# Experts in another order of work: two small mixture-of-experts layers of one transformer kernel, ordered by a table

## What is computed

```
def _hierarchical_moe(h, w_group, w_expert, w_gate, w_up, w_down):
    group = jnp.argmax(group_prob, axis=-1)                  # one of 4 groups
    top_p, top_local = lax.top_k(softmax(exp_logits), TOP_K)  # 2 of its 8 experts
    ...
    def expert_block(args):
        xb, e = args
        return (jax.nn.silu(xb @ w_gate[e]) * (xb @ w_up[e])) @ w_down[e]
    ...                                # rows of one expert at a time, then
    contrib = y[dest] * w_sorted[:, None]      # weighted sum of a token's two rows
```

## Time and profile before

| | |
|---|---|
| median of three runs | 3255.23 us |
| profiled execution, device time | 3255.2 us |
| its span, first to last instruction | 3254.0 us |
| PE busy | 2768.5 us (85%) |
| DVE, ACT, POOL busy | 1117.7, 629.0, 288.9 us |
| granted PE clock, mean | 0.923 of full speed |
| chain that ended last | PE 74%, DMA 13% (10% of it `in_w_up`), DVE 8% |

### The profile page before, as it was taken

One profiled execution on the slowest core, in us unless ns is written; L12 is line 12 of the kernel. 1 busy time (PEld: TensorE's weight loads), 2 busy tenths in 40 slices (PEclk: granted clock), 3 DMA queues, 4 the chain that ended last, 5 costly groups with the idle time before them and its releaser, 6 DMA issues.

```text
span 3254.0 us, 34233 instructions
## 1 busy us (share of the span) xinstructions
PE 2768.5 (85%) x13372; PEld 1346.5 (41%) x13372; DVE 1117.7 (34%) x2783; ACT 629.0 (19%) x1539; POOL 288.9 (9%) x379
## 2 busy tenths in 40 slices
PE   4999999998947877798949999999998478888893
PEld 3457844444443322233324444555564333232331
DVE  4225733346461111112250002777723511111124
ACT  3115600000110000001131001556512101010011
POOL 0000000000010101001020000222500101010102
PEclk9999999999968989999979999999989689899996
DMA  7221014327166789989542100001000678999994
GB/s 270 103 72 53 2 61 146 104 78 258 48 246 256 305 320 380 406 337 361 190 181 104 52 26 0 27 27 38 16 2 26 245 274 341 411 353 389 397 360 173
DMA packets 193573, 605.16 MB, mean 186 GB/s; under 512 B 52867, under 2 KB 95363, under 8 KB 176901
## 3 DMA queue, kind: packets, MB, share of 16 engines
q1 hardware_dynamic: 137076, 531.35, 42.3%
q0 software_dynamic: 56336, 71.62, 6.7%
HBM read 554.65 MB, written 47.98 MB: 185 GB/s over the span
## 4 chain that ended last, share of the span: by engine, by line
PE 74%; DMA 13%; DVE 8%; issue 3%; ACT 1%; SPq 0%; POOL 0%; DVEq 0%; POOLq 0%; ACTq 0%
PE ps L1672 16%; DMA R<-in_w_up 10%; PE ps L1645 7%; PE ps L928 7%; PE ps L2189 7%; PE ps L2621 3%; PE ps L2186 3%; PE ps L433 3%; PE ps L932 3%; PE ps L1046 3%; PE ps L439 2%; PE ps L2430 2%; PE ps L1618 2%; PE ps L2434 1%; PE ps L745 1%
## 5 line engine op out<-in xcount | busy, mean ns | idle before, releaser
L1672 PE MATMUL ps<-R 128*64 128x512 f32 (+1 forms) x3872 | 680.1, 551 | 185.2 <-issue 101.6
L1672 PEld LDWEIGHTS ps<-R 128*64 128x64 f32 (+1 forms) x3872 | 223.1, 135 | 563.5 <-issue 529.0
L1645 PE MATMUL ps<-R 128*64 128x512 f32 (+1 forms) x1936 | 309.7, 509 | 2.5 <-DVE R L1509 2.5
L928 PE MATMUL ps<-R 128*128 128x512 f32 x512 | 227.5, 604 | 0.5 <-ACT R L723 0.5
L2189 PE MATMUL ps<-R 128*128 128x512 f32 x512 | 222.2, 596 | 1.9 <-DVE R L2011 1.9
L1509 DVE COPY R<-ps 128x256 f32<-128x256 f32 (+1 forms) x97 | 38.0, 392 | 488.5 <-PE ps L1627 488.5
L1645 PEld LDWEIGHTS ps<-R 128*64 128x64 f32 (+1 forms) x1936 | 106.6, 126 | 188.5 <-issue 170.2
L1586 ACT ACTIVATE R<-ps 64x512 f32<-64x512 f32 (+1 forms) x97 | 52.5, 541 | 661.1 <-PE ps L1672 661.1
L1572 ACT ACTIVATE R<-ps,small 128x128 f32<-128x128 f32 (+1 forms) x192 | 69.8, 443 | 534.6 <-PE ps L1618 534.6
L1537 DVE TENSOR_TENSOR R<-ps,R 64x512 f32<-64x512 f32 (+1 forms) x97 | 59.8, 617 | 313.3 <-ACT R L1586 175.3
L928 PEld LDWEIGHTS ps<-R 128*128 128x128 f32 x512 | 98.9, 194 | 124.4 <-issue 123.7
(11 more groups left out here) (318 smaller groups left out, 3561.6 us busy)
## 6 DMA issues: line engine op xcount, KB each, us to landing
R<-in_w_gate SPq DMA_DIRECT2D x64, 2048.0 KB, 15.0
R<-in_w_up SPq DMA_DIRECT2D x64, 2048.0 KB, 17.7
R<-in_w_down SPq DMA_DIRECT2D x64, 2048.0 KB, 23.9
R<-in_w_ada SPq DMA_DIRECT2D x40, 1024.0 KB, 5.4
R<-in_w_in SPq DMA_DIRECT2D x13, 2048.0 KB, 8.5
YE<-R POOLq DMA_DIRECT2D x36, 256.0 KB, 19.7
R<-in_w_ada SPq DMA_DIRECT2D x4, 2048.0 KB, 16.2
XR<-in_x SPq DMA_DIRECT2D x16, 512.0 KB, 11.3
```

Of the source, the lines that this page charges most:

```text
L928: i_ = T.matmul(o, wv[:, kk, cols], k.hT[:, kk, tk], start=kk == 0, stop=kk == 7)
L1645: i_ = T.matmul(k.ps[r * j:r * j + r, 5 + b % 2, 0:n], v.hT[b % 2][:, c:c + r], v.down[m][:, kk, n * j:n * j + n], start=kk == 0, stop=kk ...
L1672: i_ = T.matmul(k.ps[P0 + r * j:P0 + r * j + r, b % 2, 0:n], x_, w[:, kk, n * j:n * j + n], start=kk == 0, stop=kk == 7)
```

## The change

The order of the experts is no longer made by the rule with `lead`; it is a table of first ranks for each layer. A group is now one rank, or two ranks where the room has an odd number of places, so that rooms of 2 places have a tile of their own. Row tiles become 32 in each layer; blocks, rooms and the place of the loop by count (before the 28th and the 27th expert) stay. In sizes the order is now 8, 2 2 3 3 2, 8, 2 1 1, 6, 2 2 2 3 3 2, 8, 2 1 1, 6, 2 3 3 1 1, loop, 4, 2 1 1 in layer 1 and 1 1 2, 6, 2 3 3 2, 4, 2 2, 6, 2 2 2 2, 8, 2 2 2 3 3, 4, 3 3 2, loop, 2 2 2 1 1 in layer 2.

```
-    def __init__(self, profile, before):
+    def __init__(self, profile, firsts, before):
...
-        groups, r = [], 0
-        while r < 31:
-            n = 2 if caps[r] % 2 else 1
-            while sum(caps[r:r + n]) < 4 and sum(caps[r:r + 2 * n]) <= 4 and r + 2 * n <= 31 and (
-                    caps[r] == caps[r + 2 * n - 1]):
-                n *= 2
-            groups.append(list(range(r, r + n)))
+        self.order, self.blocks, self.tiles, starts = [], [], [], []
+        for r in firsts:
+            g = [r, r + 1] if caps[r] % 2 else [r]
             assert base[r] % 2 == 0
-            r += n
-
-        self.order, self.blocks, self.tiles, starts, lead = [], [], [], [], 0.0
-        while groups:
-            g = groups.pop(0 if lead <= 0 or len(groups) == 1 else -1)
             starts.append(len(self.order))
-            at, end = base[g[0]], base[g[-1]] + caps[g[-1]]
+            at, end = base[r], base[g[-1]] + caps[g[-1]]
...
-                lead += 0.4 * caps[r] - 1
                 self.order.append(r)
...
+ORDER = ((0, 20, 19, 8, 13, 1, 16, 25, 4, 17, 12, 22, 6, 21, 2, 15, 27, 3, 18, 10, 23, 5, 14, 29),
...
+PLAN = [Plan(PROFILE[0], ORDER[0], None)]
+PLAN.append(Plan(PROFILE[1], ORDER[1], PLAN[0]))
```

More of the change, by code:

```diff
@@ L1424, in __init__ @@
                     u += n
-                lead += 0.4 * caps[r] - 1
                 self.order.append(r)
+        assert sorted(self.order) == list(range(31))
         self.ends = {}
@@ L1447 @@
 PROFILE = ((23, 12, 6, 5, 5, 3, 3), (27, 11, 5, 3, 3, 1, 1))
-PLAN = [Plan(PROFILE[0], None)]
-PLAN.append(Plan(PROFILE[1], PLAN[0]))
+ORDER = ((0, 20, 19, 8, 13, 1, 16, 25, 4, 17, 12, 22, 6, 21, 2, 15, 27, 3, 18, 10, 23, 5, 14, 29),
+         (27, 19, 1, 11, 5, 21, 4, 13, 18, 2, 20, 14, 16, 22, 0, 24, 15, 17, 7, 3, 9, 12, 23, 26, 25, 29))
+PLAN = [Plan(PROFILE[0], ORDER[0], None)]
+PLAN.append(Plan(PROFILE[1], ORDER[1], PLAN[0]))
 def expert_views(k):
```

## The result

The changed kernel takes 3233.51 us in the median of 20 runs (3225.41 to 3252.21), the kernel before 3254.89 us beside it: a ratio of 0.9936, 95% interval 0.992 to 0.9953. 3201 was predicted, with a range of 3180 to 3225, and 3233.5 lies above it. The profiled execution took 3230.81 us, 24.4 us less than that of before.

The account below looks back on a forecast made before the run. PE and the DMA engines, neither full, wait for each other: weight waits cost 123.4 and 105.1 us. Reordering gains 25.4 us in layer 1 and 28.7 in layer 2, 54.1 together: 3255.2 less 54.1 is 3201 us, range 3180 to 3225.

Parts of the forecast that it names:

- Row gathers become 16 more and smaller: Both expert stages: 16 more gathers, about 1.0 us of POOL issue each; taken as 0, upper bound 16 us.
- The law of the waits: Expert stages: a large room builds one fixed reserve; then weights come at the queue's pace, 17.0 us per further two-place expert.
- the walk: Expert stages: PE's time set against weight arrivals, expert by expert; waits cost 91.7 us in layer 1, 68.3 in layer 2.
- the clock: PE's first half room behind a weight wait runs slow; 1.7 us added per wait.
- none in front of a three: Sign of being right, expert stages: no weight wait stands before a three-place expert; 12 waits per layer.
- Layer 2's start: Opening experts 1 1 2 of layer 2: two new weight waits, 4.7 + 1.7 and 6.6 us, 13.0 us lost.
- The loop's wait: Layer 1, before the loop expert, which needs all three weights: a wait of some 10 us, nil in the old order.
- Rival (a): Expert stages: waits only change place, a three-place expert holding the queue 19.5 us, not 17.7; 3244 us; chance 0.11.
- Rival (b): Expert stages: the reserve is larger, waits behind three-place experts vanish and layer 2's start may hide; 3172 us; chance 0.07.
- Rival (c): Expert stages: small row tiles starve, some 43 tiles of 64 rows wait for their gathers; 3360 us; chance 0.04.
- the estimate from its figures, 10 us: Row gathers: two of 256 KB take 0.6 us more than one of 512 KB, 10 us over 16; sum 3211.
- a stage outside moving by more than a few us: Sign of being wrong: any stage outside the two expert stages moves by more than a few us.

Follow-up runs that it names:

- e5: Kernel before, each 128-row gather issued as two gathers of 128 partitions by 512 columns (wrong rows): layer 1's stage 665.7 us, before 667.8; total 3301.61 us.
- e6: Changed kernel, each 64-row tile gathered as 128 partitions by 512 columns (wrong rows): 3194.85 us, ratio 0.9819 to the kernel before.
- e10: Changed kernel, each 64-row tile gathered as two gathers of 64 partitions by 512 columns (wrong rows): 3242.41 us in one run, layer 1's stage 655.7 us.

## Why the prediction was wrong, step by step

- **The step that failed** is the sentence "Row gathers become 16 more and smaller", for which the sum took nothing, with bounds of 0 and 16 us from POOL's time to issue them. The number of gathers indeed costs nothing (e5 in layer 1), and POOL has room for them; but tiles of 64 rows, 43 for 11, slow the weight queue, and that costs 13.4 and 22.9 us, 36.3 in all (the changed kernel against its twin with wide gathers, e6; this is the price of all 43 tiles, and 39.4 us were missing in the stages). I priced the gathers on the engine that issues them and by their own landing, not by what they do to the transfers beside them. The row that hinted at it was looked at from one side only: gathers "land alike behind the weights". After, their median from issue to landing is 19.2 us over both layers (those into the `R` buffers),

```profile
R<-XN,xidx POOLq DMA_INDIRECT x56, 19.2
```

  where before it was 16.4 and with wide gathers it is 14.9, so they too were slower.
- **The law of the waits was right, in sum.** With the queue at its old pace it gives 642.4 and 583.3, and 643.6 and 585.2 were measured; the order alone gives 24.1 and 31.2 for 25.4 and 28.7. A reserve that a large room builds is the same in both orders, and a pace is what turns it into waits: at 18.8 us per expert instead of 17.5 (56.5 / 3 and 52.4 / 3) layer 1 has three waits for weights more than with wide gathers (13 and 10 in front of gate/up, the opening not counted). What the walk calls the clock shows in the profile of before: the granted clock is 0.52 over the slow half room at 1037.50 and 1.00 over the one at 1202.08. Wait by wait the law scatters: with wide gathers 7.64 us stand in front of the first three of 2 2 2 3 3 2, where 3.5 were forecast, and none in front of the large room behind it, where 3.7 were. The sign "none in front of a three" did not fit the walk itself, which puts a wait there (30.1 against 27.0, and 47.1 against 43.6).
- **Layer 2's start** came out somewhat dearer: its waits are 7.84 and 4.84 us without the clock's part, for 4.7 and 4.9 (13.0 us with the clock); with wide gathers they are 5.27 and 2.90. **The loop's wait** in layer 1 was forecast as some 10 us and is 13.1, of which the loop's opening has some 2.3; in layer 2 none was forecast and 4.6 us were measured, again with the opening's 2.3, which alone are left with wide gathers.
- **Rival (a)**, slow threes, came nearest (3244 forecast, 3231 measured in the profiled execution), and its signal was seen, in front of the second three behind the first large room. But its cause, a three's third block, is not it: experts of two places slowed too (384 GB/s in layer 2's run of them, 410 before), and with wide gathers the same three passes. **Rival (b)**, a larger reserve, is refuted: there are 13 and 14 waits in front of gate/up, not fewer than ten. **Rival (c)**, starved tiles, is refuted: each layer waits for rows once, at its start.
- **The Trainium skill** ("DMA: Bandwidth & Descriptors", section Bandwidth) pointed the right way: smaller transfers get less of the bandwidth. But the estimate from its figures, 10 us, is a third of the price, and what counted was not a transfer's size: e5 halves it and costs nothing, e10 halves the piece for one partition and gains nothing.
- **Missing from the sum** were the layers' ends: the last block has 32 rows, its store is 4.1 us shorter, twice, which is most of the 9.7 us that came outside the stages. The prediction named a stage outside moving by more than a few us as a sign that it is wrong; here it hid part of the shortfall.
- **The range** took the bounds of unknown costs only as the rows showed them. With 36 us for the gathers as a bound it would have reached 3237, and the measured time would lie within.

## What to carry to other kernels

When a change alters the shape of a small transfer, price it by what it does to the large transfers in the same DMA engines, at a stretch where these are never idle, and not only by its issue and its landing. A gather of few rows is better spread over all 128 partitions by splitting its rows into halves, if the layout is chosen when the rows are stored, so that turning them costs no extra matmuls. And when an order of work meets a law but not the time, ask which number of the law (here the pace) the change itself moved.

## What the runs showed of the hardware

- Gathers that fill 64 partitions lower what the sixteen engines move while all are busy: 402 to 383 GB/s in layer 1 of the old order when its gathers are split by rows, and 410 to 384 in layer 2 between the kernels. The same bytes by 128 partitions: 402 to 410. Over the whole stages GB/s over DMA share, good to about 2 GB/s, is 384 and 388 before, 378 and 371 after, and 389 and 393 with wide gathers. Neither which half is filled, nor the number of gathers, nor pieces of 2 KB instead of 4 KB changed that, and the packets of POOL's queue are the same 56592 with gathers of 64 rows filling 64 or 128 partitions. Why it is so stays open: no view here says which engine ran a packet.
- A float32 matmul of 64 x 64 by the identity showed two records where a transpose shows one (as the gate/up matmuls do: 16 records for the 8 of a half room): 2.13 us for the 16 of a tile, against 1.05 for 8 transposes of 64 x 128 and 0.75 for 4 of 128 x 128.
